# Re-ordering small steps of a decoder trunk on one core: the mixer's square, two gates, the key scaling, the short outputs' splits and the engine of some low parts

## What is computed

```
x += 1/2 * SwiGLU(RMSNorm(x))                       # FFN 1, inner width 2816
h = RMSNorm(x);  proj = h @ w_in                    # 1024 x 6440
y_rwkv = rwkv7(proj[0:3360])                        # width 1024, 16 heads of 64
y_sc   = rmsnorm(b_gate * conv3(c_gate * xt))       # width 512
y_ssm  = groupnorm(ssd(...) * silu(z))              # width 512
x += concat(y_rwkv, y_sc, y_ssm) @ w_out            # 2048 x 1024
x += 1/2 * SwiGLU(RMSNorm(x))                       # FFN 2
# in rwkv7:
kk = k * k_k;  kk = kk * rsqrt(max(sum_head(kk * kk), 1e-24))
a = sigmoid(a0 + a_lr @ a2);  b = kk * a
S = S * w + (S @ -kk) b^T + v k^T;  y = S @ r       # over the rows, per head
```

## Time and profile before

| | us |
|---|---|
| median of 3 runs | 1671.29 |
| lowest, highest | 1669.0, 1674.33 |
| profiled execution, its own time | 1674.05 |
| its span from first to last instruction | 1672.1 |
| mean granted TensorE clock | 0.987 of full |
| busy: PE | 1563.9 (94%) |
| busy: DVE | 993.9 (59%) |
| busy: ACT | 859.3 (51%) |
| busy: POOL | 577.7 (35%) |

### The profile page before, as it was taken

The page is one execution under the profiler, slowest core; times in us unless marked ns, Lnnn a source line. Parts: engine busy times, 40 slices in busy tenths (PEclk is TensorE's granted clock), DMA queues, the critical chain, the costliest instruction groups (busy, mean ns, idle before and its releaser), DMA issues. The chain is left out here.

```text
span 1672.1 us, 41414 instructions
## 1 busy us (share of the span) xinstructions
PE 1563.9 (94%) x17379; PEld 1483.8 (89%) x17379; DVE 993.9 (59%) x1688; ACT 859.3 (51%) x1515; POOL 577.7 (35%) x393
## 2 busy tenths in 40 slices
PE   7999999979889899999999999999897998899997
PEld 6999999977688789999999999989775887799997
DVE  5343387795798666443354434968768876654433
ACT  5444464757544555444354444657673445554443
POOL 2343403002356533444343443030115554334442
PEclk9999999999899999999999999999999999999999
DMA  7555556361244545656464655644703454356552
GB/s 228 175 167 178 169 162 201 123 205 55 55 121 119 149 137 175 199 161 200 148 185 152 202 179 176 188 143 128 213 2 99 122 164 116 127 179 200 173 188 71
DMA packets 280650, 256.28 MB, mean 153 GB/s; under 512 B 48054, under 2 KB 268700, under 8 KB 280450
## 3 DMA queue, kind: packets, MB, share of 16 engines
q1 hardware_dynamic: 276698, 252.05, 48.5%
q10 hardware_dynamic: 3768, 1.59, 0.4%
HBM read 242.22 MB, written 11.38 MB: 152 GB/s over the span
## 5 line engine op out<-in xcount | busy, mean ns | idle before, releaser
L216 POOL TENSOR_TENSOR front_lo<-front_raw,front_hi 128x1024 fp32r<-128x1024 f32 (+2 forms) x88 | 209.2, 2377 | 536.0 <-ACT front_hi L209 536.0
L209 ACT ACTIVATE front_hi<-front_raw 128x1024 fp32r<-128x1024 f32 (+2 forms) x230 | 238.4, 1038 | 269.9 <-PE ps L234 238.1
L216 POOL TENSOR_TENSOR out_lo<-out_raw,out_hi 128x1024 fp32r<-128x1024 f32 (+1 forms) x84 | 198.8, 2369 | 312.0 <-ACT out_hi L209 312.0
L209 ACT ACTIVATE out_hi<-out_raw 128x1024 fp32r<-128x1024 f32 (+1 forms) x168 | 173.2, 1038 | 213.3 <-PE ps L234 168.7
L232 PE MATMUL ps<-front_h_hi,front_hi 128*128 128x264 f32 (+1 forms) x816 | 239.6, 294 | 4.9 <-DVE front_lo L216 3.3
L216 DVE TENSOR_TENSOR front_lo<-front_raw,front_hi 128x1024 fp32r<-128x1024 f32 (+1 forms) x142 | 173.9, 1225 | 111.4 <-ACT front_hi L209 111.4
L234 PE MATMUL ps<-front_h_hi,front_lo 128*128 128x264 f32 (+1 forms) x816 | 231.5, 284 | 0.0
L233 PE MATMUL ps<-front_h_lo,front_hi 128*128 128x264 f32 (+1 forms) x816 | 231.3, 284 | 0.0
L232 PE MATMUL ps<-ffn_h_hi,out_hi 128*128 128x264 f32 x704 | 200.4, 285 | 0.1
L233 PE MATMUL ps<-ffn_h_lo,out_hi 128*128 128x264 f32 x704 | 199.6, 284 | 0.0
L234 PE MATMUL ps<-ffn_h_hi,out_lo 128*128 128x264 f32 x704 | 199.6, 284 | 0.0
(11 more groups left out here) (401 smaller groups left out, 4079.2 us busy)
## 6 DMA issues: line engine op xcount, KB each, us to landing
front_raw<-in_w_in SPq DMA_DIRECT2D x50, 1024.0 KB, 5.3
out_raw<-in_ffn_w_in SPq DMA_DIRECT2D x44, 1024.0 KB, 6.3
front_raw<-in_ffn_w_in SPq DMA_DIRECT2D x40, 1024.0 KB, 5.4
back_sample_rows<-row_scratch SPq DMA_DIRECT2D x160, 128.0 KB, 3.0
out_raw<-in_w_out SPq DMA_DIRECT2D x16, 1024.0 KB, 5.2
front_raw<-in_ffn_w_out SPq DMA_DIRECT2D x16, 896.0 KB, 4.7
out_raw<-in_ffn_w_out SPq DMA_DIRECT2D x16, 896.0 KB, 4.6
front_raw<-in_ffn_w_out SPq DMA_DIRECT2D x8, 1024.0 KB, 5.0
```

The lines of the kernel that those rows point to most:

```text
L209: act.activation(self.hi[n % self.RING][:, 0:k, 0:w], self._raw(n), ACT.Copy).then_inc(self.hi_ready, 1)
L216: eng.tensor_tensor(self.lo[n % self.RING][:, 0:k, 0:w], self._raw(n), self.hi[n % self.RING][:, 0:k, 0:w].bitcast(F32), ALU.subtract).the ...
```

## The change

No product and no DMA is added or removed. It does the following:

1. ACT's square of the short convolution (line 1047) moves from behind the outer products of m = 3 to ahead of them.
2. In the front stage DVE instead of POOL makes the low parts of tiles 40 and 42.
3. The gates of p = 6 and 7 run one tile earlier on PE (slots 46, 47) and ACT (47, 48); DVE cumulates p = 6 and 7 in slots 48 and 49.
4. `normed_keys(1)` and `minus_b(1)`, the keys of pairs 4 to 7, leave the front stage. There remain the eight sample columns (`key_samples`, slot 50); the 256 prompt columns are scaled by DVE in g = 1 of the back stage, between `start(1)` and the bonus lines. POOL's `weigh(4)` waits for them. The norms' buffer stays where it was, and is now known to both stages (`mix.nrm`).
5. The splits of the short outputs are spread in g = 7: ACT has one after `tokens(7, 0)`, one after `t1_copy(6, 2)`, one before `t1_copy(6, 4)` and one after `state_copy(5, 2)`; POOL has one where it had three, and three where it had one (ahead of `level(7, 0)`).
6. In the output projection DVE makes the low parts of halves 8, 10, 12 and 14 too.

```diff
@@ front_stage
-    *range(base + 4, base + 14, 2), *range(base + 26, base + 39, 2),
+    *range(base + 4, base + 14, 2), *range(base + 26, base + 43, 2),
...
                     for m in range(4):
                         yield 27 + 2 * m + m // 2
+                        if m == 3:
+                            act.wait_ge(s("sc_gated"), 1)
+                            act.wait_ge(s("bc_ps"), 4)
+                            act.activation(sq, acc, ACT.Square).then_inc(s("sc_sq"), 1)
                         act.wait_ge(s("xs_dt"), 1)
...
-                    act.wait_ge(s("sc_gated"), 1)
-                    act.wait_ge(s("bc_ps"), 4)
-                    act.activation(sq, acc, ACT.Square).then_inc(s("sc_sq"), 1)
                     yield 37
...
-                    for p, slot in enumerate((40, 41, 42, 43, 44, 45, 48, 49)):
+                    for p, slot in enumerate((40, 41, 42, 43, 44, 45, 47, 48)):
...
+                    def key_samples():
+                        c = slice(4, RT)
+                        dve.wait_ge(s("norm_inv"), 1)
+                        dve.wait_ge(s("fac_done"), RT)
+                        dve.tensor_tensor(mix.kkn[:, c, T:N], mix.kkn[:, c, T:N], nrm[:, c, T:N], ALU.mult).then_inc(s("kkn_done"), 1)
+                        dve.wait_ge(s("kkn_done"), 2)
+                        dve.scalar_tensor_tensor(out=mix.nb[:, c, T:N], in0=mix.kkn[:, c, T:N], scalar=-1.0, in1=mix.nb[:, c, T:N],
+                                                 op0=ALU.mult, op1=ALU.mult).then_inc(s("nb_done"), 1)
...
-                        if slot in (47, 49, 50):
-                            cumulate({47: 5, 49: 6, 50: 7}[slot])
+                        if slot in (47, 48, 49):
+                            cumulate(slot - 42)
...
-                        if slot == 49:
-                            normed_keys(1)
                         if slot == 50:
-                            minus_b(1)
+                            key_samples()
...
-                        if slot < 45 or 47 <= slot < 49:
-                            p = slot - 39 if slot < 45 else slot - 41
+                        if slot < 45 or 46 <= slot < 48:
+                            p = slot - 39 if slot < 45 else slot - 40
@@ back_stage
-        ws = Stream(st, KT, pieces, halves, raw_ring=3, buffers=(
+        ws = Stream(st, KT, pieces, halves, raw_ring=3, on_dve={*range(8, OUT_HALVES, 2), *range(1, len(halves), 2)}, buffers=(
... pool, weigh(p)
+                    if p == 4:
+                        pool.wait_ge(s("late_keys"), 2)
... pool, loop over g
                     if g == RT - 1:
-                        for q in range(3):
-                            short_split_lo(q)
+                        short_split_lo(0)
...
                     if g == RT - 1:
-                        short_split_lo(3)
+                        for q in range(1, 4):
+                            short_split_lo(q)
                     if g < RT:
                         level(g, 0)
... scalar, loop over g, each under "if g == RT - 1"
                         short_split_hi(0)
-                        short_split_hi(1)
                     if 0 <= l < RT:
                         t1_copy(l, 2)
-                        short_split_hi(2)
-                        short_split_hi(3)
+                        short_split_hi(1)
...
                         state_copy(c, 1)
+                        short_split_hi(2)
                         t1_copy(l, 4)
                         rv_copy(l)
                         state_copy(c, 2)
+                        short_split_hi(3)
... vector, loop over g
                     if g < RT:
                         start(g)
+                    if g == 1:
+                        c = slice(4, RT)
+                        dve.tensor_tensor(mix.kkn[:, c, 0:T], mix.kkn[:, c, 0:T], mix.nrm[:, c, 0:T], ALU.mult).then_inc(s("late_keys"), 1)
+                        dve.wait_ge(s("late_keys"), 1)
+                        dve.scalar_tensor_tensor(out=mix.nb[:, c, 0:T], in0=mix.kkn[:, c, 0:T], scalar=-1.0, in1=mix.nb[:, c, 0:T],
+                                                 op0=ALU.mult, op1=ALU.mult).then_inc(s("late_keys"), 1)
... vector, behind y_split_lo of pairs 5 to 7
+                ws.split_lo(dve, 8)
                 ws.split_lo(dve, 9)
                 for mt in range(KT):
-                    if mt % 2 == 0 and mt:
-                        ws.split_lo(dve, 9 + mt)
+                    if mt % 2 == 0:
+                        if mt:
+                            ws.split_lo(dve, 9 + mt)
+                        if mt < KT - 2:
+                            ws.split_lo(dve, 10 + mt)
```

More of the change, by code:

```diff
@@ L863, in front_stage @@
         wa2, g2, g2b = at("w2_a2", 0, [P, D]), at("g2", 4096, [P, D]), at("g2_tail", 8192, [32, D])
-        nrm = at("kk_norm", 20736, [P, RT, N])
+        nrm = mix.nrm
         rk = at("r_k", 65216, [P, 2, N])
@@ L1559, in mix_stages @@
             mix.ar0, mix.vecs = place("first_a_r", 74592, [P, 2, T]), place("sample_vecs", 72768, [P, RT, 5, NS])
+            mix.nrm = place("kk_norm", 20736, [P, RT, N])
             mix.root, mix.sc_root = place("ssm_root", 68608, [P, 2, N]), place("sc_root", 76640, [P, N])
@@ L1772, in _ @@
                 for n in range(4, OUT_HALVES, 2):
-                    ws.split_lo(pool, n)
+                    if not ws.on_dve[n]:
+                        ws.split_lo(pool, n)
                 ffn.pool(pool)
@@ L1935, in _ @@
                         state_copy(c, 1)
+                    if g == RT - 1:
+                        short_split_hi(2)
                     if 0 <= l < RT:
```

## The result

| | before | after |
|---|---|---|
| median, us | 1672.0 | 1693.93 |
| lowest, highest | 1669.0, 1674.33 | 1692.43, 1694.86 |
| profiled execution, its span | 1674.05, 1672.1 | 1692.43, 1690.4 |
| mean granted TensorE clock | 0.987 | 0.977 |
| busy: PE | 1563.9 | 1573.4 |

The kernel after is slower: its time is 1.0131 of the time before, 95% interval 1.0117 to 1.0145. That is 22 us where 9.4 were forecast, and outside the range given. Between the two profiled executions, a long one of the kernel before and the shortest of the kernel after, it is 18.4 us, of which PE's own busy time, with the same products, makes 9.5: so half of the loss isn't waiting but slower work.

The account below looks back on a forecast made before the run. PE was taken as the bound, busy 1563.9 of 1672.1 us, so only its pauses and clock could move. Terms -2.1 + 2.6 + 0.8 + 2.5 + 0.6 + 0.3 = +4.7 us a layer, +9.4 in all: 1680.7 us, range 1669 to 1687.

Parts of the forecast that it names:

- the pause at the transposes: PE, having finished tile 37 early, stands 5.5 us ahead of line 1468, waiting for DVE's read of the sum.
- the pause at p = 6: PE stands 4.5 us in place of 1.25 in slot 46, until ACT has evicted the gates of p = 5.
- The DVE tail: End of the front stage: DVE's work after tile 48 falls from 15.3 to 12.7 us.
- DVE's last instruction of the front stage: Sign to look for in the trace: it ends some 0 to 1 us later than before.
- Line 1468: Sign at PE's transposes: the prediction is wrong if this line does not come 2 us earlier.
- step 2: Gates of p = 6 and 7 one tile earlier: front stage ends 2.6 us later, plus 0.8 for the clock, a layer.
- step 1: Square ahead of the outer products, tiles 40 and 42 on DVE: -2.1 us a layer, with 0.7 taken for the clock.
- Layer 1 shows the same waits: Assumption from the list of PE's waits: terms worked out for layer 0 hold in layer 1, so each sum is doubled.
- The filled wait at p = 6: Rival denying this wait in slot 46: PE finds the gates of p = 5 evicted; 1668.5 us, chance 0.06.
- Both clock prices in full: Rival: slower clock behind both new pauses costs its upper bound, +8.5 us a layer, 1688 us; chance 0.08.
- POOL's blocking: Rival at the output projection: waits for DVE's low parts go, -4.1 us a layer instead of +0.3; 1671.9 us, chance 0.10.
- The additions hide: Rival: later pauses absorb DVE's time in g = 1 and the late POOL step; 1672.5 us, chance 0.16.

Follow-up runs that it names:

- u_keys: The kernel after with the late keys alone undone (keys of pairs 4 to 7 scaled in full in the front stage): 1692.21 us, ratio 1.0124 to the kernel before.
- gates runs: Two runs: the kernel after with only the earlier gates of p = 6 and 7 undone, 1679.84 us; the kernel before with only them, 1688.53 us.
- fill: The kernel after with ten unused products added on PE ahead of its wait at p = 6: 1689.16 us, ratio 1.0101 to the kernel before.
- u_outlow: The kernel after with POOL again making the even low parts of the output projection: 1694.31 us, ratio 1.0132 to the kernel before.
- only_gates: The kernel before with only the gates of p = 6 and 7 moved one tile earlier: 1688.53 us, ratio 1.0096.

## Why the prediction was wrong

**What held.** The direction, and each of the waits that the forecast put in place of an old one, in layer 0: the pause at the transposes (5.5 forecast, 5.98 measured), the pause at p = 6 ended by ACT (4.5 and 4.46), the first `solve` (3.7 and 3.39), POOL's level at the first step of g = 8 (1.74 us in layer 0), the low part of half 8 (a pause of 2.03 us, where half 8 was to be 1.2 later). The DVE tail was forecast at 12.7 us from the end of tile 48 (about 434.8) and took 12.9, by luck as to its parts: with the keys in full it takes 14.7 in `u_keys` and not 15.3, and the late keys take 1.8 off it and not 2.6. DVE's last instruction ended at 447.65 (447.22 + 0.43), and the back stage began at 448.95 where it had begun at 443.11. The late keys took 2.2 us in g = 1 where 2.5 were booked: this is the growth of the shift from the back stage's start, +5.8, to the first `solve`, +8.0. From there to g = 9, where the splits lie, the shift of layer 0 fell from +8.0 to +6.2 (608.19 to 614.42 at half 7), against +0.6 forecast; the output projection took 1.9 us (+6.2 to +8.1), against +0.3. The two errors, -2.4 and +1.6, largely cancel, by luck. In layer 1 the same two stretches took +0.7 (9.3 to 9.9 at half 7) and +0.4, near the forecast. These are differences of two traces; no run shows them to be the price of the splits or of the low parts.

Two of the forecast's own signs failed. DVE's last instruction of the front stage was to come 0 to 1 us later (its sum gives 1.3) and came 5.85 later (441.80 to 447.65). Line 1468 was to come 2 us earlier, and did so in layer 0 (3.2 us), but not in layer 1 (1.0).

**The step that failed: the price of the clock, the second part of step 2 and the last of step 1.** Step 1 booked 0.7 us for it and step 2 booked 0.8, with at most 1.7 each. Both ends came from one row, the 0.57 of the earlier trace rows, which shows a short fall behind a pause of 5.15 us. Measured in layer 0 behind the transposes: the 3.2 us gained at their start have shrunk to 0.7 by the LoRA products of p = 2 (389.8 to 389.1), so 2.4 us (the pause on the way, 0.56 us, is the same in both kernels); behind the pause at p = 6, 14.9 less 11.0, so 3.9 us. That is 6.3 us in place of 1.5, a layer, and both above the upper end of 1.7. The gates runs, the fill run and the stretches show for p = 6 that it is the clock: 8 us of uninterrupted work at half clock are 4 us of work at full clock. For the 2.4 us at the transposes the stretch at 0.62 is the evidence, and no run that takes the clock's fall away there. The error in method is that a bound was taken from the one stretch where the clock had fallen, with its length, and the length is what changes. The kernel before has a longer one, 0.50 from 439 to 446 behind a pause of only 3.66 us, and the forecast didn't use it.

**The step that was doubled wrongly.** "Layer 1 shows the same waits" rested on the list of waits, which has two pauses for the square. The pause ahead of the transposes, 2.31 us, is there in layer 0 alone. Layer 1 of the kernel before:

```profile
1188.22 0.60 PE L1468 MATMUL ps<-cst,sc_new 128*18 128x128 f32 x4
```

No pause stands in the bracket. So the gain at the transposes was 1.0 us there, not 2.8 (table above), and the fall of the clock made it a loss: by the products of p = 2 layer 1 was 0.6 us behind.

**The sum again.** With -0.7 for step 1 in layer 0 and +0.6 in layer 1 in place of -2.1, and +3.9 in place of +0.8 for the clock at p = 6, the forecast of +9.4 becomes 9.4 + 1.4 + 2.7 + 2 x 3.1 = 19.7 us, against 18.4 between the profiled executions and 22 between the medians.

**The rivals.** The filled wait at p = 6 isn't absent: 4.46 us of it. "Both clock prices in full" was the right mechanism, at 0.08 and 1688 us, and still too small by the same bound. "POOL's blocking" at the output projection fell: giving POOL's parts back changed nothing (`u_outlow`). Its mechanism is real, though: DVE's step of 0.43 us took 2.50 beside POOL's low part, but the low part that DVE makes instead costs as much. "The additions hide" was not borne out: the 2.2 us of the late keys in g = 1 stand in the table, and beside edit 3 they are nearly paid back by DVE's shorter tail, which step 2 had booked.

**What stays open.** Why the clock comes back after a short stretch behind one pause and after a long one behind another of about the same length (5.15 us and 4.46 us) isn't settled. PE's work behind the second one is largely small products of the gates and bonus sums; whether that matters wasn't tried. The length of the pause alone doesn't decide it. The last bonus sums of the kernel before in layer 1 are

```profile
1259.39 1.16 PE L1508 MATMUL ps<-r_k,cst 128*128 128x264 f32 x4 [3.65 <-DVE r_k L1302]
```

and in layer 0, behind 3.66 us, the same four products took 2.13 us, at half clock. The pauses of 2.03 and 1.99 us at half 8 differ in the same way. The fall at p = 6, though, is there in both layers (the first product behind the pause took 0.81 and 0.80 us). Nor is the stretch at half clock that appeared behind the first `solve` in `fill` explained.

## What to carry to other kernels

A pause taken away can turn up at the next wait of the same engine, as here; before booking the gain, follow the engine to the next wait and ask who is late there, in every repetition of the loop. When an edit creates a pause of several microseconds on TensorE, price the work behind it at half clock for as long as the longest such stretch in the trace, not the shortest, as the upper bound, and nothing as the lower: the same pause had a fall behind it in one layer and none in the other. An engine's product should be asked for only after the engine that feeds it has passed its own longest chain: here the gates one tile earlier cost 14 to 17 us.

## What was not expected of the hardware

- The granted clock was 0.50 for eight microseconds in which PE had no pause at all (8.00 us busy of 8.00, `only_gates` 0.51), behind a pause of 4.46 us; ten unused products in that pause kept it at 1.00. The Trainium skill tells of such falls at DMA waits that recur with each tile (TensorE: Matmul & The Clock Gate, HAM oscillation — how this bites in real kernels) and advises to restructure the loop so that TensorE stays at its full clock. The waits here are for ACT and DVE, and the trace agrees in that the clock falls behind them, to 0.50; by `fill` unused products in the wait keep it up too, at a price of their own.
- The same pause had a fall of the clock behind it or not: 2.03 us gave 0.62 (622 to 626 us) and 1.99 us gave 1.00 (1456 to 1460 us) in one execution.
- At half clock a busy PE looks as busy as before: its busy time rose by 9.5 us with the same products. The share of busy time can't tell work from slow work.
- A DVE addition of 1024 columns took 3.08 us beside a POOL operation of 2.93 us and 1.22 without it.
